# Two orders of issue in a fused two-block kernel: ScalarE's copies of the transposed probabilities set before the exponentials, and a broadcast matmul of the mLSTM core moved one unit ahead

## The chip, the cores and the metric

One core of one Trainium2 chip runs the whole program. The metric is the device time of one execution in microseconds (us); of the kernel before, the median of three runs is 4267.76 us (4265.85 to 4268.33).

The core has engines that run their own instruction streams and meet at semaphores: PE (TensorE, matrix products and transposes into PSUM), DVE (VectorE), ACT (ScalarE), POOL (GpSimd) and SP, which issues the loads from memory. Each engine starts its compute instructions in the order of its own stream; a wait at one instruction therefore holds back what stands behind it.

## The reference, cut to what matters

The input is 512 tokens of width 1024. A first block (a state-space branch, an RWKV branch, an HGRN branch, a feed-forward) runs once, then two layers of a second block. Each of those two layers has four branches on the normalised tokens, a gated merge, an output projection and a feed-forward. The change touches only the cores of the four branches:

```python
# A: mLSTM, 4 heads of 128, both directions, chunks of 128
dmat = where(lower, b[t] - b[s] + i[s], -inf);  mt = max(b + m, dmat.max(-1))
h = (q @ k.T * exp(dmat - mt)) @ v / max(abs(den), exp(-mt))        # forward + backward, then normed

# B: grouped-query attention, 8 heads of 64, 512 queries x 512 keys
p = softmax(q @ k.T);            o = p @ v
# C: neighbourhood attention, 8 heads, a window of 8 x 16 positions, with a bias table
p = softmax(q @ k.T + bias);     o = p @ v
# D: differential attention, 4 heads, two maps, a distance bias
a = softmax(s0) - lam * softmax(s1);   o = a @ v
```

Everything is held in 32-bit floats.

## The kernel before, in words

The program is a chain of stages. Long projection stages stream weights through SP and keep PE nearly full. Between them stand short stages without any weights, which work on tiles already in SBUF and PSUM; four of them per layer are meant here: the mLSTM core, and the cores of the grouped-query, differential and neighbourhood attentions (built by `gqa_attention`, `diff_attention`, `natten_branch`; each runs through `alone`, that is with nothing else beside it).

**An attention core** is a software pipeline over steps n. In a step, a block of 128 queries of two heads (and, in the differential one, of one of two maps) is handled. PE's stream for step n is: the scores of step n into PSUM (L3118, in the neighbourhood core L3379), then the transposes of the probabilities of an earlier pair (L3128, L3390), then the product with the values for one pair earlier still (L3140, L3401). DVE finds the row maxima of step n ("front": L3197; with a bias L3203 and L3208; L3449 and L3454), and then normalises step n-1 (L3175 to L3187; L3435, L3439). ACT computes the two exponentials of step n (L3156, L3415) and copies the transposed probabilities of the earlier pair from PSUM banks 4 and 5 into `prob_t` (L3163, L3423); this copy is called the take below. In the code m numbers the pairs whose probabilities are transposed, and m = n - 2, except in the differential core, where two maps make one m and it exists for every second n only.

The waits that tie these together: the scores of step n need the exponentials (or the front) of n-2 done; the transposes of m need its normalisation and the take of m-1, because they write the banks that the take reads; the values' product needs the take of m; the exponentials of n need the front of n; the take of m needs the transposes of m and the values' product of m-2. There are 16 steps in each of the three cores; the differential one has 8 transposed pairs.

**The mLSTM core** (`mlstm_branch`, L2922 on) runs 32 steps s in 8 units u of four (`NT` = 4); a unit is one head in one direction. At each unit's start PE spreads the unit's row of running maxima over all partitions with one 4x512 matmul into bank u % 2 ("spread", L2951). Per step: DVE bounds (spread value minus a column, L3031), ACT takes the exponential (L2991), POOL masks the diagonal block (L2971), PE makes the products of queries and keys (L2955), DVE multiplies the two ("weight", L3005), and PE multiplies that with the values ("weigh", L2933). In PE's stream, step s is: spread if s % 4 is 0, the query-key product of s (which needs the weight of s-2), weigh of s-2. In DVE's stream it is: bound of s, weight of s-2, and at s % 4 = 3 the closing of the previous unit (`finish`). The blocks of a unit have 512, 384, 256 and 128 columns, in this order.

The order of the work is written out in the source; no scheduler moves it.

Of the kernel before, what the change touches and what calls it, by code (L numbers as in the profile page):

```python
# [18 lines left out]
ACT = mybir.ActivationFunctionType  # L19
AX = mybir.AxisListType  # L20

P = 128
T = 512
NT = T // P
# [294 lines left out]
def bank(ps, b):  # L319
    return ps[:, b, :]  # L320
# [297 lines left out]
class Nothing:  # L618
# [10 lines left out]
    def scalar(self, act):  # L629
        yield  # L630
# [2241 lines left out]
def mlstm_branch(k, n_layer, y, o_gate, norm):  # L2872
# [7 lines left out]
    H, N, PAD = A_HEADS, 2 * A_WIDTH // P, A_CONV // 2  # L2880
    n = n_layer
    with ExitStack() as ctx:
# [8 lines left out]
        b_, g_, M_, m_ = [sb(name, [H, 2, T]) for name in ("b_rows", "g_rows", "max_rows", "m_rows")]  # L2891
        g_col, m_col = sb("g_cols", [P, NT, 2, H]), sb("floor_cols", [P, NT, 2, H])
        stat = sb("row_scale", [P, 2, NT])
# [5 lines left out]
        with ExitStack() as inner:  # L2899
# [8 lines left out]
            UNITS = 2 * H  # L2908
            STEPS = UNITS * NT

            def place(s):

                u = s // NT
                back, h = u % 2, u // 2
                j = NT - 1 - s % NT if back else s % NT
                return u, back, h, j, (slice(0, (j + 1) * P) if back else slice(j * P, T))

            def values(u, i):

                return k.ps[:, 4 + 2 * (u % 2) + i // 2, (i % 2) * (P + 1):(i % 2) * (P + 1) + P + 1]  # L2920

            @block.tensor  # L2922
            def _(pe):
                def weigh(s):
                    u, back, h, j, ts = place(s)
                    pe.wait_ge(prob_ready, s + 1)
                    if s % NT == 0 and u >= 2:
                        if back:
                            pe.wait_ge(y_ready, h)
                        else:  # L2930
                            pe.wait_ge(first_half, NT * h)
                    for i in range(0, j + 1) if back else range(j, NT):
                        mm = pe.matmul(values(u, i), dist[:, s % RING, i * P:(i + 1) * P], v_one[:, j, h, :],  # L2933
                                       start=(s % NT == 0 and i % 2 == 0), stop=(j == (0 if back else i)),
                                       skip_group_check=True)
                    mm.then_inc(pv_done, 1)

                def turn(h):

                    pe.wait_ge(both_halves, NT * (h + 1))  # L2940
                    for i in range(NT):
                        mm = pe.transpose(k.ps[:, 6, i * P:(i + 1) * P], tap[:, h % 2, i * P:(i + 1) * P],
                                          k.const("ident"))
                    mm.then_inc(turned, 1)

                for s in range(STEPS):
                    u, back, h, j, ts = place(s)
                    if s % NT == 0:
                        if u >= 2:
                            pe.wait_ge(bounded, NT * (u - 1))  # L2950
                        pe.matmul(bank(k.ps, u % 2), k.const("ident", H)[:, h:h + 1].broadcast_to([H, P]),  # L2951
                                  M_[:, back, :], start=True, stop=True).then_inc(spread, 1)
                    if s >= 2:
                        pe.wait_ge(prob_ready, s - 1)
                    pe.matmul(k.ps[:, 2 + s % 2, ts], qk[:, H + h, j * P:(j + 1) * P], qk[:, h, ts],  # L2955
                              start=True, stop=True).then_inc(qk_done, 1)
                    if s >= 2:
                        weigh(s - 2)
                    if s % NT == 0 and u >= 3 and back:
                        turn(h - 1)  # L2960
                weigh(STEPS - 2)
                weigh(STEPS - 1)
                turn(H - 1)
# [106 lines left out]
class Attention(Nothing):  # L3070
# [74 lines left out]
    def scalar(self, act):  # L3145
        k, stat = self.k, self.stat
        for n in range(self.N + 2):
            if n < self.N:
                g, i, c = self.place(n)
                act.wait_ge(self.fronts, self.front * (n + 1))  # L3150
                if n >= self.RE and self.bias_of is None:
                    act.wait_ge(self.turned, (n - self.RE) // self.maps + 1)
                for s in range(2):
                    at, e = 2 * (n % 4) + s, self.exp[:, n % self.RE, s, :]
                    src = bank(k.ps, 2 * (n % 2) + s) if self.bias_of is None else e
                    act.activation(e, src, ACT.Exp, bias=stat[:, 0, at:at + 1],  # L3156
                                   accum_out=stat[:, 1, at:at + 1]).then_inc(self.exps, 1)
            m = self.done(n - 2)
            if m is not None:
                act.wait_ge(self.turned, m + 1)  # L3160
                if m >= 2:
                    act.wait_ge(self.pv_done, m - 1)
                act.activation(self.pt[:, m % 2, :, :, :],  # L3163
                               k.ps[:, 4:6, :].rearrange("p s (j t) -> p s j t", j=NT), ACT.Copy).then_inc(self.taken, 1)
            yield

    def vector(self, dve):
# [172 lines left out]
class WindowAttention(Nothing):  # L3340
# [66 lines left out]
    def scalar(self, act):  # L3407
        k, stat = self.k, self.stat
        for n in range(self.N + 2):
            if n < self.N:  # L3410
                g, b, lo, w = self.place(n)
                act.wait_ge(self.fronts, 3 * (n + 1))
                for s in range(2):
                    at, e = 2 * (n % 4) + s, self.exp[:, n % self.RE, s, 0:w * P]
                    act.activation(e, e, ACT.Exp, bias=stat[:, 0, at:at + 1], accum_out=stat[:, 1, at:at + 1])\  # L3415
                        .then_inc(self.exps, 1)
            m = n - 2
            if m >= 0:
                g, b, lo, w = self.place(m)
                act.wait_ge(self.turned, m + 1)  # L3420
                if m >= 2:
                    act.wait_ge(self.pv_done, m - 1)
                act.activation(self.pt[:, m % 2, :, 0:w, :],  # L3423
                               k.ps[:, 4:6, 0:w * P].rearrange("p s (j t) -> p s j t", j=w), ACT.Copy)\
                    .then_inc(self.taken, 1)
            yield

    def vector(self, dve):
# [353 lines left out]
```

## Time and profile before

| | before |
|---|---|
| median of 3 runs | 4267.76 us |
| lowest, highest | 4265.85, 4268.33 us |
| profiled execution, its own time | 4268.34 us |
| its span | 4266.5 us |
| mean granted TensorE clock in it | 0.939 of full |
| PE busy | 3839.9 us (90%) |
| DVE busy | 2026.0 us (47%) |
| ACT busy | 1525.0 us (36%) |
| POOL busy | 399.8 us (9%) |

All times below are from that one execution. A busy share is a mean over stages with different limits, so the table says only that PE is the fullest engine of the program as a whole; the short stages have to be read one by one. In the profile a number in square brackets behind an instruction is the idle time of its engine just before it, with what ended it. Matrix products are pipelined and their ends are modelled; the distance between two starts is the better measure. A 32-bit product counts as two matmul records or more.

### The profile page before, as it was taken

The page shows a single profiled execution, that of the slowest core. Times are in us where ns is not written, and L with a number is a line of the kernel's source. Part 1 is how long each engine was busy: PE and PEld are TensorE (multiplying, and loading weights), DVE is VectorE, ACT ScalarE, POOL GpSimd, SP SyncE. Part 2 cuts the span into 40 slices and gives each one's busy share as a digit, 9 for nine tenths or more (in the row PEclk, how much of TensorE's full clock was granted, in tenths as well). Part 3 has the DMA queues.
Part 4 walks back from the last instruction along what each step waited for, and adds up shares of the span by engine and source line. Part 5 has one row for each costly group of instructions (what it writes and reads, how often), then busy time and mean ns, then how long its engine had stood idle before and what let it go on. Part 6 is the DMA issues. An engine that isn't in the chain of part 4 may idle for free. (4 is left out here: it accounts for less than half of the span.)

```text
span 4266.5 us, 51904 instructions
## 1 busy us (share of the span) xinstructions
PE 3839.9 (90%) x20480; PEld 2973.0 (70%) x20480; DVE 2026.0 (47%) x3134; ACT 1525.0 (36%) x2371; POOL 399.8 (9%) x356
## 2 busy tenths in 40 slices
PE   7888778969999998989789999999989789999998
PEld 5456667757878876766567877877766567777876
DVE  4867464485343333536546443333436645443332
ACT  4443312543332233424444332232424444233232
POOL 0025223000001103010000001100010000001100
PEclk9999778979999998999999999999999999999999
DMA  3011001202322222111112332222211112332222
GB/s 107 15 50 48 1 2 36 84 1 74 121 86 95 94 78 72 60 50 40 69 43 86 91 96 89 93 78 81 70 45 45 40 66 88 90 98 85 95 77 74
DMA packets 83486, 289.30 MB, mean 68 GB/s; under 512 B 9168, under 2 KB 9296, under 8 KB 82000
## 3 DMA queue, kind: packets, MB, share of 16 engines
q1 hardware_dynamic: 83136, 286.30, 20.9%
q8 instruction: 141, 2.31, 0.2%
q14 instruction: 65, 0.53, 0.0%
q10 hardware_dynamic: 144, 0.15, 0.0%
HBM read 284.32 MB, written 2.10 MB: 67 GB/s over the span
## 5 line engine op out<-in xcount | busy, mean ns | idle before, releaser
L547 DVE TENSOR_TENSOR weights_lo_r<-raw_weights,weights_hi_r 128x1024 fp32r<-128x1024 f32 (+2 forms) x554 | 633.0, 1143 | 1758.1 <-ACT weights_hi_r L541 1757.9
L541 ACT ACTIVATE weights_hi_r<-raw_weights 128x1024 fp32r<-128x1024 f32 (+2 forms) x554 | 548.0, 989 | 1856.8 <-PE ps L614 1821.3
L613 PE MATMUL ps<-xn_r,weights_hi_r 128*128 128x512 f32 x2816 | 1118.8, 397 | 0.0
L612 PE MATMUL ps<-xn_hi,weights_hi_r 128*128 128x512 f32 x1952 | 805.6, 413 | 74.4 <-DVE xn_r L607 27.3
L614 PE MATMUL ps<-xn_hi,weights_lo_r 128*128 128x512 f32 x1952 | 777.4, 398 | 0.0
L613 PEld LDWEIGHTS ps<-xn_r,weights_hi_r 128*128 128x128 f32 x2816 | 539.0, 191 | 126.7 <-issue 10.6
L612 PEld LDWEIGHTS ps<-xn_hi,weights_hi_r 128*128 128x128 f32 x1952 | 377.1, 193 | 193.9 <-issue 82.5
L614 PEld LDWEIGHTS ps<-xn_hi,weights_lo_r 128*128 128x128 f32 x1952 | 377.1, 193 | 83.6
L612 PE MATMUL ps<-y_r,weights_hi_r 128*128 128x512 f32 x1056 | 420.9, 399 | 1.6 <-PEq L858 1.6
L614 PE MATMUL ps<-y_r,weights_lo_r 128*128 128x512 f32 x1056 | 420.2, 398 | 0.0
L612 PE MATMUL ps<-hidden_hi,weights_hi_r 128*128 128x512 f32 x528 | 216.1, 409 | 31.9 <-DVE hidden_r L607 31.9
L612 PEld LDWEIGHTS ps<-y_r,weights_hi_r 128*128 128x128 f32 x1056 | 199.4, 189 | 50.6 <-issue 4.0
L614 PEld LDWEIGHTS ps<-y_r,weights_lo_r 128*128 128x128 f32 x1056 | 199.7, 189 | 49.3
L613 PE MATMUL ps<-hidden_r,weights_hi_r 128*128 128x512 f32 x528 | 214.9, 407 | 0.0
L614 PE MATMUL ps<-hidden_hi,weights_lo_r 128*128 128x512 f32 x528 | 214.3, 406 | 0.0
L1156 POOL TENSOR_TENSOR squares<-squares 128x512 f32<-128x512 f32 x18 | 23.2, 1291 | 1852.6 <-ACT squares L1145 1852.6
L612 PE MATMUL ps<-y_hi,weights_hi_r 128*128 128x512 f32 x384 | 157.1, 409 | 0.0
L614 PE MATMUL ps<-y_hi,weights_lo_r 128*128 128x512 f32 x384 | 151.9, 396 | 0.0
L613 PE MATMUL ps<-y_r,weights_hi_r 128*128 128x512 f32 x384 | 151.9, 396 | 0.0
L3627 POOL TENSOR_TENSOR y<-y 128x512 f32<-128x512 f32 x66 | 85.2, 1291 | 675.2 <-ACT y L3599 675.2
L612 PEld LDWEIGHTS ps<-hidden_hi,weights_hi_r 128*128 128x128 f32 x528 | 103.0, 195 | 60.6 <-DVE weights_lo_r L547 20.0
L614 PEld LDWEIGHTS ps<-hidden_hi,weights_lo_r 128*128 128x128 f32 x528 | 102.9, 195 | 25.3
(490 smaller groups left out, 5340.0 us busy)
## 6 DMA issues: line engine op xcount, KB each, us to landing
raw_weights<-in_w_ffn_dram SPq DMA_DIRECT2D x132, 512.0 KB, 3.7
raw_weights<-in_w_down_dram SPq DMA_DIRECT2D x48, 512.0 KB, 3.5
raw_weights<-in_w_out_dram SPq DMA_DIRECT2D x24, 512.0 KB, 3.5
bias_table<-in_window_bias_dram SPq DMA_DIRECT2D x8, 1280.0 KB, 10.5
raw_weights<-in_w_down_dram SPq DMA_DIRECT2D x24, 384.0 KB, 3.1
raw_weights<-in_w_hgrn_dram SPq DMA_DIRECT2D x16, 512.0 KB, 3.5
raw_weights<-in_w_mix_ssm_dram SPq DMA_DIRECT2D x16, 512.0 KB, 3.7
raw_weights<-in_w_a_qk_dram SPq DMA_DIRECT2D x16, 512.0 KB, 3.4
```

The lines of the kernel that those rows point to most:

```text
L541: act.activation(self.k.w_hi[:, g % 2, 0:chunk.width], self.k.raw[:, slot, 0:chunk.width], ACT.Copy)\
L547: dve.tensor_tensor(self.k.w_lo[:, g % 2, 0:chunk.width], self.k.raw[:, slot, 0:chunk.width], self.k.w_hi[:, g % 2, 0:chunk.width].bitcast ...
L612: pe.matmul(out, w_hi, x_hi, start=start, stop=False)
L613: pe.matmul(out, w_hi, x_lo, start=False, stop=False)
L614: return pe.matmul(out, w_lo, x_hi, start=False, stop=stop)
L1156: pool.tensor_tensor(self.sums[:, n, :], self.sums[:, n, :], self.sq[:, kinds * (m % 2) + n, :], ALU.add)\
L3627: pool.tensor_tensor(gate[:, s, :], gate[:, s, :], rstd, ALU.mult).then_inc(gate_scaled, 1)
```

## The change

Two edits.

In both attention classes, `scalar` (ACT's stream) has its two parts exchanged inside a step: first the take of m, then the exponentials of step n. Nothing else in the two classes changes, neither a wait nor a number that is waited for.

In the mLSTM core the spread of unit u+1 is issued in the middle of unit u, behind the weigh of s - 2 at s % 4 = 2, and no longer in front of the first query-key product of unit u+1. The spread of unit 0 stands before the loop. The wait for the bank's last reader (`bounded`) goes along.

```diff
+                def spread_maxima(u):
+                    if u >= 2:
+                        pe.wait_ge(bounded, NT * (u - 1))
+                    pe.matmul(bank(k.ps, u % 2), k.const("ident", H)[:, u // 2:u // 2 + 1].broadcast_to([H, P]),
+                              M_[:, u % 2, :], start=True, stop=True).then_inc(spread, 1)
+
+                spread_maxima(0)
                 for s in range(STEPS):
                     u, back, h, j, ts = place(s)
-                    if s % NT == 0:
-                        if u >= 2:
-                            pe.wait_ge(bounded, NT * (u - 1))
-                        pe.matmul(bank(k.ps, u % 2), k.const("ident", H)[:, h:h + 1].broadcast_to([H, P]),
-                                  M_[:, back, :], start=True, stop=True).then_inc(spread, 1)
                     if s >= 2:
                         pe.wait_ge(prob_ready, s - 1)
                     pe.matmul(k.ps[:, 2 + s % 2, ts], qk[:, H + h, j * P:(j + 1) * P], qk[:, h, ts],
                               start=True, stop=True).then_inc(qk_done, 1)
                     if s >= 2:
                         weigh(s - 2)
+                    if s % NT == 2 and u + 1 < UNITS:
+                        spread_maxima(u + 1)
...
     def scalar(self, act):
         k, stat = self.k, self.stat
         for n in range(self.N + 2):
+            m = self.done(n - 2)
+            if m is not None:
+                act.wait_ge(self.turned, m + 1)
+                if m >= 2:
+                    act.wait_ge(self.pv_done, m - 1)
+                act.activation(self.pt[:, m % 2, :, :, :],
+                               k.ps[:, 4:6, :].rearrange("p s (j t) -> p s j t", j=NT), ACT.Copy).then_inc(self.taken, 1)
             if n < self.N:
                 g, i, c = self.place(n)
                 act.wait_ge(self.fronts, self.front * (n + 1))
...
-            m = self.done(n - 2)
-            if m is not None:
-                act.wait_ge(self.turned, m + 1)
-                if m >= 2:
-                    act.wait_ge(self.pv_done, m - 1)
-                act.activation(self.pt[:, m % 2, :, :, :],
-                               k.ps[:, 4:6, :].rearrange("p s (j t) -> p s j t", j=NT), ACT.Copy).then_inc(self.taken, 1)
             yield
```

The same exchange is made in `WindowAttention.scalar`, with the take of w blocks instead of four.

On ACT, at the start of the first grouped-query core (L3156 the exponentials, two to a step; L3163 the take), the kernel before has:

```order
L3156 ACTIVATE exps,statistics<-ps,statistics 128x512 x6
L3163 ACTIVATE prob_t<-ps 128x1024
L3156 ACTIVATE exps,statistics<-ps,statistics 128x512 x2
L3163 ACTIVATE prob_t<-ps 128x1024
L3156 ACTIVATE exps,statistics<-ps,statistics 128x512 x2
```

and the changed one, in which the exponentials are L3167 and the take is L3157:

```order
L3167 ACTIVATE exps,statistics<-ps,statistics 128x512 x4
L3157 ACTIVATE prob_t<-ps 128x1024
L3167 ACTIVATE exps,statistics<-ps,statistics 128x512 x2
L3157 ACTIVATE prob_t<-ps 128x1024
L3167 ACTIVATE exps,statistics<-ps,statistics 128x512 x2
```

The first take stands behind the exponentials of two steps instead of three, and every later one has moved ahead of one step's pair of exponentials.

On PE, around the boundary between the first and the second unit of the mLSTM core (L2951 the spread, L2955 the query-key products, L2933 the weigh), the kernel before has:

```order
L2955 MATMUL ps<-qk 128x256
L2933 MATMUL ps<-v_tok,qk_raw 128x129 x4
L2955 MATMUL ps<-qk 128x128
L2933 MATMUL ps<-v_tok,qk_raw 128x129 x3
L2951 MATMUL ps<-max_rows,consts 128x512
L2955 MATMUL ps<-qk 128x512
L2933 MATMUL ps<-v_tok,qk_raw 128x129 x2
```

and the changed one (L2949 the spread, L2957 the query-key products):

```order
L2957 MATMUL ps<-qk 128x256
L2933 MATMUL ps<-v_tok,qk_raw 128x129 x4
L2949 MATMUL ps<-max_rows,consts 128x512
L2957 MATMUL ps<-qk 128x128
L2933 MATMUL ps<-v_tok,qk_raw 128x129 x3
L2957 MATMUL ps<-qk 128x512
L2933 MATMUL ps<-v_tok,qk_raw 128x129 x2
```

The spread has moved up past one 128-column product and three weigh products, which now stand between it and the 512-column product.

## Rows read from the trace of the kernel before

**Rows 1.** Windows; columns: stretch, length, busy (xcount) of PE, PEld, DVE, ACT, POOL, PEclk, DMA share, GB/s
```profile
1819.50:1822.50 3.00, 3.00 (x10) 2.20 (x9) 1.92 (x8) 0.31 (x1) 0.94 (x3) 0.50 0.00 0
1990.00:2036.00 46.00, 40.75 (x366) 26.14 (x364) 30.63 (x57) 31.82 (x70) 0.00 (x0) 1.00 0.01 1
2066.00:2068.00 2.00, 2.00 (x10) 1.77 (x10) 0.00 (x0) 0.00 (x0) 0.00 (x0) 0.50 0.00 0
2073.11:2087.49 14.38, 10.39 (x65) 6.64 (x65) 11.13 (x31) 7.81 (x18) 0.00 (x0) 1.00 0.00 1
2199.78:2210.38 10.60, 8.66 (x77) 5.42 (x77) 7.90 (x35) 7.15 (x20) 0.00 (x0) 1.00 0.01 2
```

**Rows 2.** Timeline, mLSTM core, a unit boundary; columns: start, length, engine, line, instruction
```profile
1793.32 0.39 PE L2955 MATMUL ps<-qk 128*128 128x128 f32 x2
...
1794.30 1.12 PE L2951 MATMUL ps<-max_rows,consts 4*128 4x512 f32 x2
1795.46 0.75 DVE L3031 TENSOR_SCALAR qk_raw<-ps,g_cols 128x512 f32<-128x512 f32 x1 [2.64 <-PE ps L2951]
1796.13 0.41 DVE L3005 TENSOR_TENSOR qk_raw<-qk_raw,ps 128x256 f32<-128x256 f32 x1
...
1796.59 1.12 PE L2955 MATMUL ps<-qk 128*128 128x512 f32 x2 [1.17 <-DVE qk_raw L3005]
```

**Rows 3.** Timeline, PE alone, later unit starts of the mLSTM core
```profile
1803.47 1.13 PE L2955 MATMUL ps<-qk 128*128 128x512 f32 x2 [1.17 <-DVE qk_raw L3005]
...
1817.96 1.13 PE L2955 MATMUL ps<-qk 128*128 128x512 f32 x2 [1.17 <-DVE qk_raw L3005]
1826.51 1.12 PE L2955 MATMUL ps<-qk 128*128 128x512 f32 x2 [1.17 <-DVE qk_raw L3005]
```

**Rows 4.** Timeline, grouped-query core, two steps
```profile
1999.21 1.07 PE L3128 MATMUL ps<-consts,exps 128*128 128x128 f32 x8 [0.71 <-ACT prob_t L3163]
...
2002.32 1.07 PE L3128 MATMUL ps<-consts,exps 128*128 128x128 f32 x8
...
2003.67 0.69 ACT L3156 ACTIVATE exps<-ps,statistics 128x512 f32<-128x512 f32 x1 [1.50 <-DVE statistics L3197]
...
2005.01 1.02 ACT L3163 ACTIVATE prob_t<-ps 128x1024 f32<-128x1024 f32 x1
...
2005.52 1.23 DVE L3197 TENSOR_REDUCE statistics<-ps 128x2 f32<-128x1024 f32 x1 [0.89 <-PE ps L3118]
...
2006.18 1.07 PE L3128 MATMUL ps<-consts,exps 128*128 128x128 f32 x8 [0.70 <-ACT prob_t L3163]
```

**Rows 5.** Who waited for the take (us, times), both layers: L3163
```profile
  PE ps L3140: 28.1, 14
  PE ps L3128: 13.5, 18
```

**Rows 6.** The same for the neighbourhood core's take: L3423
```profile
  PE ps L3390: 13.7, 22
```

**Rows 7.** Timeline, differential core, one pair of steps
```profile
2076.27 0.69 DVE L3203 CUSTOM_DVE_ANT_0 exps<-ps,distance_bias 128x512 f32<-128x512 f32 x1 [1.49 <-PE ps L3118]
...
2079.24 1.00 ACT L3163 ACTIVATE prob_t<-ps 128x1024 f32<-128x1024 f32 x1
...
2080.30 2.05 PE L3140 MATMUL ps<-prob_t,d_v 128*128 128x128 f32 x16 [2.00 <-ACT prob_t L3163]
...
2080.56 1.42 DVE L3187 SCALAR_TENSOR_TENSOR exps<-exps,statistics 128x512 f32<-128x512 f32 x2
```

**Rows 8.** Timeline, PE alone, differential core: the products with the values of two earlier pairs
```profile
2064.32 3.24 PE L3140 MATMUL ps<-prob_t,d_v 128*128 128x128 f32 x16 [1.99 <-ACT prob_t L3163]
2073.11 2.05 PE L3140 MATMUL ps<-prob_t,d_v 128*128 128x128 f32 x16 [2.00 <-ACT prob_t L3163]
```

**Rows 9.** What DVE's fronts of the differential cores waited for (us, times): L3203
```profile
  PE ps L3118: 25.8, 16
```

**Rows 10.** Timeline, neighbourhood core, the transposes that open a group of four steps
```profile
2199.78 0.63 PE L3390 MATMUL ps<-consts,exps 128*128 128x128 f32 x4 [1.02 <-ACT prob_t L3423]
```

More of the change, by code:

```diff
@@ L3409, in scalar @@
         for n in range(self.N + 2):
[L3410 to L3416, printed above, removed]
             m = n - 2
@@ L3425, in scalar @@
                     .then_inc(self.taken, 1)
+            if n < self.N:
+                g, b, lo, w = self.place(n)
+                act.wait_ge(self.fronts, 3 * (n + 1))
+                for s in range(2):
+                    at, e = 2 * (n % 4) + s, self.exp[:, n % self.RE, s, 0:w * P]
+                    act.activation(e, e, ACT.Exp, bias=stat[:, 0, at:at + 1], accum_out=stat[:, 1, at:at + 1])\
+                        .then_inc(self.exps, 1)
             yield
```

## The prediction, made before the changed kernel was run

> **What bounds the kernel now.** I began with the table of engines and the forty slices: PE is 90% busy over the whole, but the slices with the low digits are those in which almost nothing is loaded. Those are the cores without weights, and the edits touch only them. So I went on to the windows [rows 1]. In the steady part of the grouped-query core PE works 40.75 of 46 us; in the differential core 10.39 of 14.38, in the neighbourhood core 8.66 of 10.60. All three have free time on every engine at once (DVE 30.63, 11.13, 7.90), which means a ring of waits and not a full engine. The timelines then say which wait ends last.
>
> In the mLSTM core it is the start of a unit [rows 2]: the spread starts at 1794.30, DVE has stood idle 2.64 us for it, bounds at 1795.46, weights at 1796.13, and only then may PE go on, at 1796.59, after 1.17 us of idleness. The same 1.17 us stand before the first product of each of the 14 units that follow another unit (7 in each layer) [rows 2, 3].
>
> In the grouped-query core [rows 4] PE has transposed by 2002.32 + 1.07 = 2003.4, but the take starts at 2005.01, because ACT first runs the exponentials of the step, which could start only at 2003.67. The next transposes, at 2006.18, have waited 0.70 us for that take, as every second one does. In the differential core the product with the values waits 2.00 us [rows 7]; in the neighbourhood core transposes wait, 1.02 us at most and 1.94 us in a group of four steps, the stretch's 10.60 minus PE's 8.66 [rows 1, 10].
>
> **The change, part by part.** No instruction is added and none is removed; no DMA, no queue of SP or POOL is passed. The sums below are waits that go.
>
> *mLSTM core.* The chain from the spread's start to the 512-column product is 1796.59 - 1794.30 = 2.29 us [rows 2], and the change keeps it: DVE's bound still needs the spread, its weight still follows the bound. But one 128-column product and three weigh products now run inside it. Before, they ran from 1793.32 to 1794.30, 0.98 us [rows 2]. The spread itself occupies PE about as long as from 1794.30 to 1796.59 less the idle 1.17, so 1.12. PE is then ready at 1.12 + 0.98 = 2.10, the chain at 2.29: about 0.2 us of the 1.17 stays. Saved: 0.98 per boundary, 14 x 0.98 = 13.7 us. What is late next is DVE's closing of a backward unit, which stands before the bound; I followed one such boundary through and it frees DVE within 0.1 us of the spread's end, so I charge nothing. If that cover is gone, its cost is a few tenths at 6 boundaries, 2 us. The bounds are 0 (if the middle of a unit has no slack for the spread) and 14 x 1.17 = 16.4.
>
> *The clock in that core.* From 1819.50 to 1822.50 the granted clock is 0.50, that is 1.2 GHz instead of 2.4 [rows 1], and the unit in it takes 1826.51 - 1817.96 = 8.55 us against 1803.47 - 1796.59 = 6.88 for one of its size [rows 2, 3]: 1.67 us for a dip. Three units of the two layers show one. In the differential core a dip stands between 2064.32 and 2073.11, 8.79 us against 7.19 for the next pair (2080.30 - 2073.11): 1.6 us [rows 7, 8], four of them in steady state. In the grouped-query core the granted clock is 1.00 throughout 46 us in which PE is 89% busy [rows 1]. With the waits gone, both other cores come to that density or above it: in the mLSTM core only 0.2 us in some 5.9 stay idle. I count two of the three dips there as gone: 2 x 1.67 = 3.3 us, with the bounds 0 and 5.0.
>
> *Grouped-query core.* The take moves to where the transposes end. The exponentials then start after it: transposes' end 2003.4 + 1.02 = 2004.4 instead of 2003.67, 0.75 us later. They are needed by DVE's normalisation, which stands behind the next front. The exponentials end at 2005.8 (they took 2005.01 - 2003.67 = 1.34); DVE's next front waits for the next scores and runs from 2005.52 to 2006.75, so 0.9 us of slack is left. PE becomes the bound, with (6.97 - 0.70) / 2 = 3.13 us a step. ACT's own load is 1.34 + 1.02 = 2.36, below it. The waits before L3128 sum to 13.5 us in 18 places [rows 5]. The last of each layer, 1.02 and 0.18, stand where no exponentials are left and stay: 11.0 us. Bounds 0 and 13.5.
>
> *Differential core.* PE waits 28.1 us in 14 places [rows 5], but PE is not what decides here once the take is early. DVE does four things for a pair: from 2076.27 to the end of L3187, 2080.56 + 1.42 = 2081.98, it works without a gap for 5.71 us, and waits 1.49 before it [rows 7]. PE needs, with rows 8's distance, 7.19 - 2.00 = 5.19. So a pair falls from 7.19 to 5.71. The fronts' waits in both layers sum to 25.8 us in 16 places [rows 9]; I leave out some 5 us for the filling of the pipeline, in which nothing has been transposed yet, and 1.6 us for one dip that stays: 19.2 us. The slack in the ring is thin. With X the end of L3187, transposes run to about X + 1.2 (1.07 and a start), the take to X + 2.2 (1.00), the exponentials to X + 3.6 (1.34, rows 4). DVE wants them when front, normalisation and front are done, which is 5.71 less the 1.42 of L3187 and some 0.45 of small work before it, X + 3.8. Bounds 14.4 (all four dips stay) and 22.8 (the filling costs 3 instead of 5).
>
> *Neighbourhood core.* PE waits 13.7 us in 22 places [rows 6]. PE needs 8.66 us for a group of four steps and DVE, waits inside it left out, 7.90 [rows 1]; with the small gaps between dependent instructions I add up 8.3. The margin is 0.4 us a group. I take 10.0 us, with the bounds 0 and 12.5 (the 13.7 without those of the tails and of a start at half clock).
>
> Sum: 13.7 + 3.3 + 11.0 + 19.2 + 10.0 = 57.2 us. The profiled execution took 4268.34 us, of which 4266.5 are its span; that is 0.6 above the median of the runs, so the median becomes 4267.8 - 57.2 = 4211 us, 1.3% less.
>
> A rule of the Trainium skill speaks against the exchange. What the trace shows first: the take stands 1.6 us behind the end of its transposes, with ACT at work on what precedes it in the stream [rows 4]. "TensorE: Matmul & The Clock Gate", Part 1, says that ScalarE and VectorE take their instructions strictly first in, first out. The trace agrees. By that rule the exchange has its price: the exponentials now cannot pass a take that waits for PE. That price is the 0.75 us above; it costs nothing while the slack of 0.9 us holds, and by the rule alone, without slack, it would be 0.75 x 16 x 2 = 24 us in the grouped-query core.
>
> **The rivals.** *The clock keeps its dips.* For it: dips also stand behind stretches whose PE work is mostly transposes and small products, and these stay. Against it: the grouped-query core, with the same transposes, has none in 46 us [rows 1]. Price: 3.3 us in the mLSTM core, and in the differential core 19.2 - 14.4 = 4.8. Time 4211 + 8.1 = 4219.
>
> *The thin margins fail.* DVE or ACT becomes the bound in the neighbourhood core, with latencies that I have not seen between take and exponentials: 0.4 us a step less gained there over 16 steps in two layers takes all 10.0, and 0.3 us in each of some 12 pairs of the differential core takes 3.6. Time 4211 + 13.6 = 4225. For it: ACT's 7.15 us of a group are 1.8 of a step that would be 8.66 / 4 = 2.17, and each of its two waits adds a start. Against it: nothing says that these starts take more than the 0.4 left.
>
> *Covered.* Something else sets the pace of those stages, and the time stays at 4268. Only a record that names the wrong releaser could bring this; the take and the waiting transposes line up to 0.15 us [rows 4], in each of 18 places.
>
> *Slower.* The exponentials, held behind a take that waits for PE, close a ring at half clock. At 0.50 each PE step doubles from 3.13 to 6.26 us, the take and with it the exponentials come later by the same factor, so all cores run at PE's half pace. Place: the grouped-query core, whose steady part shows no dip now. Price: 3.13 us a step. It takes 57.2 / 3.13 = 18 of its 32 steps at half clock to lose all of the gain; with all 32, 100 us are lost and the time is 4311. For it: the clock does fall in cores of this kind [rows 1]. Against it: it fell where PE was idle more, and the change makes it idle less.
>
> **How the numbers follow.** Chances: my forecast 0.60, dips kept 0.18, margins fail 0.15, covered 0.03, slower 0.04. The forecast's own range is 4203 to 4216: with all dips gone and nothing lost the terms are 13.7 + 5.0 + 11.8 + 22.8 + 12.5 = 65.8, which gives 4202. The range that holds 8 in 10 goes from there through both middle cases and a little past the second: 4202 to 4227. About 0.2%, 8.5 us, is what a measurement of this kernel can tell from no change; faster by more than that are the first three cases, 0.93; same 0.03; slower 0.04.
>
> **What would show it right or wrong.** In the profile of the changed kernel: (1) the idle before the 512-column query-key product falls from 1.17 to about 0.2, and a unit's start follows the last one after some 5.9 us instead of 6.88; (2) in the grouped-query core no transposes wait for the take in steady state, and their distance is 3.13 us; (3) in the differential core the fronts no longer wait for PE, and a pair takes 5.7 us; (4) the neighbourhood core's group takes 8.7 to 9.0 us; (5) the granted clock is 1.00 in steady state in all four. It is wrong if exponentials are now what DVE waits for, if (3) stays above 6.3, or if stages outside these eight change by more than 1 us.

## The result, and the profile after

| | before | after |
|---|---|---|
| median | 4266.81 us (4 runs) | 4189.91 us (4 runs) |
| lowest, highest | 4260.96, 4268.33 | 4186.72, 4195.19 |
| profiled execution, its own time | 4268.34 | 4195.19 |
| its span | 4266.5 | 4193.4 |
| mean granted TensorE clock | 0.939 | 0.943 |

The ratio is 0.983, with the 95% interval 0.981 to 0.984: faster, by 77 us. I had predicted 4211 with the range 4202 to 4227; the time lies 12 us below its low end. The sign was right, the size was not.

The profiled executions differ by 73.15 us. I cut both at the borders of the stages. The eight cores account for 69.35 us of it, all other stages together for 3.8. For each core, in us: its length; the time in it in which PE is not busy; and the time at half clock, worked out as 2 x (1 - granted clock) x length. A stretch at half clock is called a dip. The granted clock is printed with two digits, so the last figure is good to about 0.6 us (2 x 0.005 x 60): 7.4 against 6.7, or 3.8 against 3.4, is no difference. In the trace's own record of the clock the grouped-query cores have 6.8 and 3.2 us of half clock in both orders.

| core (layer) | length | PE not busy | half clock | shorter by | forecast, both layers |
|---|---|---|---|---|---|
| mLSTM (1) | 62.77 to 55.40 | 11.05 to 3.37 | 7.5 to 5.5 | 7.4 | |
| mLSTM (2) | 66.12 to 56.05 | 11.05 to 3.37 | 14.6 to 7.8 | 10.1 | 17.0, was 17.4 |
| grouped-query (1) | 61.51 to 55.41 | 8.69 to 2.83 | 7.4 to 6.7 | 6.1 | |
| grouped-query (2) | 61.30 to 54.63 | 9.52 to 3.09 | 3.7 to 3.3 | 6.7 | 11.0, was 12.8 |
| differential (1) | 69.89 to 57.17 | 20.05 to 12.88 | 21.0 to 6.9 | 12.7 | |
| differential (2) | 66.97 to 56.43 | 20.05 to 12.88 | 13.4 to 3.4 | 10.5 | 19.2, was 23.3 |
| neighbourhood (1) | 47.77 to 39.47 | 9.26 to 5.03 | 10.5 to 0 | 8.3 | |
| neighbourhood (2) | 47.05 to 39.47 | 10.88 to 5.04 | 3.8 to 0 | 7.6 | 10.0, was 15.9 |

The cores of layer 1 in the windows before (mLSTM, grouped-query, differential, neighbourhood; columns as in [rows 1]):

```profile
1787.71:1850.48 62.77, 51.72 (x256) 35.29 (x257) 37.50 (x104) 22.06 (x53) 14.30 (x32) 0.94 0.00 1
1982.23:2043.74 61.51, 52.82 (x448) 33.43 (x449) 37.37 (x68) 39.27 (x81) 0.00 (x0) 0.94 0.00 1
2043.74:2113.63 69.89, 49.84 (x257) 32.91 (x257) 46.88 (x140) 31.53 (x72) 0.00 (x0) 0.85 0.00 1
2182.92:2230.69 47.77, 38.51 (x304) 24.06 (x305) 31.67 (x132) 28.98 (x81) 0.00 (x0) 0.89 0.00 1
```

and after, followed by one group of four steps of the neighbourhood core and one pair of the differential core:

```profile
1788.06:1843.46 55.40, 52.03 (x256) 35.02 (x257) 37.44 (x104) 22.01 (x53) 14.25 (x32) 0.95 0.00 1
1973.93:2029.34 55.41, 52.58 (x448) 33.41 (x449) 37.53 (x68) 39.14 (x81) 0.00 (x0) 0.94 0.00 1
2029.34:2086.51 57.17, 44.29 (x257) 28.17 (x257) 46.49 (x140) 31.58 (x72) 0.00 (x0) 0.94 0.00 1
2155.73:2195.20 39.47, 34.44 (x305) 21.83 (x305) 31.18 (x132) 29.55 (x81) 0.00 (x0) 1.00 0.01 1
2170.48:2179.47 8.99, 8.60 (x77) 5.42 (x77) 7.72 (x34) 7.38 (x21) 0.00 (x0) 1.00 0.00 1
2051.28:2056.89 5.61, 5.26 (x33) 3.32 (x33) 5.43 (x18) 3.95 (x9) 0.00 (x0) 1.00 0.00 0
```

The reader should compare PE's busy column. The instructions are the same, yet PE is busy 5.55 us less in the differential core and 4.07 us less in the neighbourhood core: the same products took less time, because less of them ran at half clock. Such a gain is not a wait that goes; it stands in no list of waits.

In the mLSTM core the boundary that answers to [rows 2] reads, in the timeline:

```profile
1800.89 1.12 PE L2949 MATMUL ps<-max_rows,consts 4*128 4x512 f32 x2
1801.94 0.49 PE L2957 MATMUL ps<-qk 128*128 128x128 f32 x2
1802.05 0.75 DVE L3035 TENSOR_SCALAR qk_raw<-ps,g_cols 128x512 f32<-128x512 f32 x1 [1.49 <-PE ps L2949]
...
1802.71 0.41 DVE L3009 TENSOR_TENSOR qk_raw<-qk_raw,ps 128x256 f32<-128x256 f32 x1
...
1803.18 1.13 PE L2957 MATMUL ps<-qk 128*128 128x512 f32 x2
```

The chain from the spread's start is 1803.18 - 1800.89 = 2.29 us, as before to the hundredth. PE now works inside it; the bracket with 1.17 us is gone. The next unit starts at

```profile
1809.16 1.13 PE L2957 MATMUL ps<-qk 128*128 128x512 f32 x2
1815.59 1.12 PE L2957 MATMUL ps<-qk 128*128 128x512 f32 x2
```

so 5.98 and 6.43 us for the two kinds of unit; in [rows 2, 3] the first kind took 6.88, and both together 14.49 (1817.96 - 1803.47), now 12.41.

A step of the grouped-query core:

```profile
2001.68 1.09 PE L3132 MATMUL ps<-consts,exps 128*128 128x128 f32 x8
2001.80 1.22 DVE L3201 TENSOR_REDUCE statistics<-ps 128x2 f32<-128x1024 f32 x1 [0.89 <-PE ps L3122]
...
2002.81 1.02 ACT L3157 ACTIVATE prob_t<-ps 128x1024 f32<-128x1024 f32 x1 [0.75 <-PE ps L3132]
...
2003.73 0.68 ACT L3167 ACTIVATE exps<-ps,statistics 128x512 f32<-128x512 f32 x1
...
2004.78 1.09 PE L3132 MATMUL ps<-consts,exps 128*128 128x128 f32 x8
```

The step is 3.10 us and no transpose waits. ACT now waits 0.75 us for PE before the take. The exponentials behind it become ready while the take runs, at 2003.02, where their front (started at 2001.80) ends, and start at 2003.73. In this step nobody waits for them. In the whole profile the normalisations wait for exponentials in 6 places, 4.0 us together (before: 4 places, 1.5 us); none of the 6 lies in a steady stretch.

A stretch of the differential core:

```profile
2056.75 0.68 DVE L3207 CUSTOM_DVE_ANT_0 exps<-ps,distance_bias 128x512 f32<-128x512 f32 x1
2056.89 1.09 PE L3132 MATMUL ps<-consts,exps 128*128 128x128 f32 x8 [0.29 <-DVE exps L3191]
...
2058.02 1.02 ACT L3157 ACTIVATE prob_t<-ps 128x1024 f32<-128x1024 f32 x1 [1.41 <-PE ps L3132]
...
2059.10 2.05 PE L3144 MATMUL ps<-prob_t,d_v 128*128 128x128 f32 x16
```

The take that [rows 7] have at 2079.24, 1.06 us ahead of the product that waited 2.00 us for it, now follows the transposes at once. DVE's front has no bracket: the list of what the fronts (L3207) waited for has 6.1 us in 6 places, where [rows 9] have 25.8 in 16. DVE is busy 5.43 of 5.61 us and is what bounds the pair.

### The profile page after: what moved, and what is told of

Same layout as the page of the kernel before. It is cut to its first block and busy times, and to the rows that moved or that the text cites. A ratio compares the mean times of both kernels' runs of the same rounds, so it can differ in the third digit from the quotient of the medians.

```text
span 4193.4 us, 51904 instructions
## 1 busy us (share of the span) xinstructions
PE 3822.6 (91%) x20480; PEld 2960.6 (71%) x20480; DVE 2024.4 (48%) x3134; ACT 1524.8 (36%) x2371; POOL 399.6 (10%) x356
## 5 line engine op out<-in xcount | busy, mean ns | idle before, releaser
L1156 POOL TENSOR_TENSOR squares<-squares 128x512 f32<-128x512 f32 x18 | 23.3, 1294 | 1797.2 <-ACT squares L1145 1797.2
```

What stands on the lines that cost most here:

```text
L1156: pool.tensor_tensor(self.sums[:, n, :], self.sums[:, n, :], self.sq[:, kinds * (m % 2) + n, :], ALU.add)\
```

## The experiments

Two theories stood at first. **A**: each core's gain is its own, namely the waits that went and, where PE is fuller, the full clock that it then keeps. **B**: the half clock has nothing to do with the waits; it comes and goes by chance or with the stage, and the excess over the forecast is something else.

### One core at a time: e1, e2, e3, e4

Each starts from the kernel before and takes one part of the change. e1 has only the hunk of `mlstm_branch`. In e2 and e3 the attention class asks which core it is (one map: grouped-query, two: differential), and e4 changes `WindowAttention.scalar` alone:

```diff
         for n in range(self.N + 2):
+            if self.maps == 1:          # e2; in e3: self.maps == 2
+                take(n)
             ...                         # the exponentials of n
+            if not (self.maps == 1):
+                take(n)
```

> The mLSTM edit alone, the three attention cores as before. Theory A (each core's gain is its own: fewer waits, and a fuller PE that keeps the full clock in that core): the two mLSTM cores lose 15.4 us of PE idle time and about 2 us of half clock, together 17 us, and the six attention cores keep their old idle time (8.7 to 20.1 us each) and, on average, their old half clock (before: 21.0 and 13.4 us in the differential cores, 10.5 and 3.8 in the neighbourhood ones). Total 4250 us. Theory B (half clock comes and goes by chance from one execution to the next, whatever the order of the work): untouched cores show 0 half clock in some of them, the neighbourhood cores above all, and the total may be anywhere within 4245 to 4256.

> The exchange of take and exponentials in the grouped-query core alone. Theory A: these two cores lose 12.3 us of PE idle time, half clock in them stays where it was (at their start), the others are as before; total 4267 - 12.5 = 4254 us. Theory B: the same for the idle time, and the untouched cores' half clock scatters, down to 0 in some. Under both, transposes of this core follow each other by 3.13 us in steady state, and the differential core behind it is no shorter than 66 us.

> The exchange in the differential core alone. Theory A: idle time falls by 14.3 us in the two cores and the half clock in each falls from 21.0 and 13.4 us to below 8, which is worth another 8.9 us of PE time; together 23 us, total 4244 us. Theory B: the idle time falls by 14.3 us, and the half clock falls only by chance: 4 to 20 us remain in a core, and the total is 4246 to 4253.

> The exchange in the neighbourhood core alone. Theory A: idle time falls by 10.1 us and the half clock goes from 10.5 and 3.8 us to 0 in both cores, 16 us together, total 4251 us, and both cores take 39.5 us. Theory B: the idle time falls by 10.1 us, some half clock shows in at least one of the two cores, and the total is 4253 to 4257.

| | median, us | ratio (95%) | its two cores | shorter by | half clock there |
|---|---|---|---|---|---|
| e1 | 4236.0 | 0.994 (0.992 to 0.996) | 54.97, 56.05 | 17.9 | 4.4, 7.8 |
| e2 | 4247.2 | 0.996 (0.995 to 0.997) | 54.63, 55.41 | 12.8 | |
| e3 | 4235.9 | 0.994 (0.992 to 0.996) | 57.49, 57.58 | 21.8 | 6.9, 6.9 |
| e4 | 4248.8 | 0.997 (0.996 to 0.998) | 39.47, 39.48 | 15.9 | 0, 0 |

The before on that chip had a median of 4266.3. "Shorter by" is against the cores of the profile of before. Its sum is 68.4; the whole change gave 69.35. So the gains of the cores add up, and each stands in the core whose order was changed.

Part of what B says is true all the same. In untouched cores the half clock moves between profiles too: e2's first differential core had 10.7 us instead of 21.0 (66.95 us long instead of 69.89), e3's first neighbourhood core 3.8 instead of 10.5, e4's second mLSTM core 7.6 instead of 14.6. A single pair of profiles can't price the clock. All profiles together can. The old order had 10.7 to 21.1 us of half clock in ten differential cores, the new one 3.4 to 6.9 in twelve (e7's, which have spare products, left out); in the neighbourhood core it is 3.8 to 10.5 in eight against 0 in eleven of twelve. These ranges do not meet, and no untouched core of the two kinds came down to 0, which is against B. In the mLSTM core they just meet: 7.4 to 15.4 in twelve against 4.9 to 7.7 in eight (from the clock's record). With the mean over all profiles of either order in place of the one pair (kernels that alter a core in some other way are left out for that core), the eight cores give 68.6 us instead of 69.35: 52.8 of PE's time not busy, and 15.8 of its busy time (mLSTM 3.1, grouped-query 0.4, differential 7.8, neighbourhood 4.4).

The medians did not come out as A had them: they lie 14, 7, 8 and 2 us below its totals (4250, 4254, 4244, 4251). Nor do they add up: 30.3 + 19.1 + 30.4 + 17.5 = 97.3 for a whole of 77. The profiles show one reason for unsteady totals: the stretch of the first block from about 262 us on, 700 us long and touched by no edit, took 716.9 us in the profile of before, 716.7 after, and 714.4, 707.6, 710.0 and 707.7 in e1 to e4. It goes with half clock: by the clock's record the two longest of these stretches had 249.5 and 254.0 us of it, those of e2 and e4 233.5. What makes the half clock differ there I did not find. Cores are therefore compared by their lengths, in which e6, a repeat of the changed kernel, differs from it by 0.4 us at most. The old order scatters more: its ten differential cores took 66.95 to 70.21 us, its twelve mLSTM cores 62.77 to 66.63.

### The clock by itself: e5

The kernel before, with spare products into banks that nothing reads before they are overwritten, at places where PE waits. The order of takes and exponentials stays, so the waits for the take stay.

```diff
+                if maps == 2:                 # differential: ahead of the wait for the take
+                    for r in range(6):
+                        pe.matmul(self.out(2 * g + r % 2)[:, i * P:(i + 1) * P], self.v_of(2 * g + r % 2, 0), k.const("ident"), start=True, stop=True)
                 pe.wait_ge(self.taken, m + 1)
...
+                if n >= 3:                    # neighbourhood: four products of 128 columns, behind the scores
+                    ...
```

> The kernel before, with spare products put into PE's idle time: four 128-column ones in each step of the neighbourhood core, between the scores and the transposes, and six in each pair of the differential core, ahead of the wait for the take; their results are overwritten. All waits and the order of the real work stay. They add about 0.5 us of PE time to a step and 1.5 us to a pair, in places where PE stands idle. Theory A (the clock falls where PE stands idle much, and the part of the gain that the removed waits don't explain is the clock that the fuller PE keeps): half clock falls from 3.8-10.5 us to 0 in each neighbourhood core, and from 10.7-21.1 to below 8 in each differential one; the differential cores get shorter by 3 to 5 us each in spite of the added work (67-70 to 64-66), the neighbourhood cores by 0 to 4. Theory B (the clock has nothing to do with it, the waits alone made the gain): no core gets shorter, half clock stays at the values of before, and the added work makes the cores 0 to 3 us longer.

Median 4258.0 against 4263.6, ratio 0.998 (0.997 to 0.999). The differential cores took 66.78 and 66.68, with 6.7 us of half clock each, where the old order had 10.7 to 21.1 in ten cores of five profiles. The pair stayed at 7.18 us. Windows of that core and the neighbourhood core of e5:

```profile
2037.41:2104.19 66.78, 55.51 (x352) 39.69 (x353) 46.88 (x140) 31.50 (x72) 0.00 (x0) 0.95 0.00 1
2173.43:2221.67 48.24, 44.71 (x408) 28.74 (x409) 31.67 (x132) 28.93 (x81) 0.00 (x0) 0.93 0.01 2
```

and PE's timeline:

```profile
2059.46 2.05 PE L3147 MATMUL ps<-prob_t,d_v 128*128 128x128 f32 x16 [0.45 <-ACT prob_t L3170]
2066.64 2.05 PE L3147 MATMUL ps<-prob_t,d_v 128*128 128x128 f32 x16 [0.46 <-ACT prob_t L3170]
```

The reader sees PE 5.67 us busier than before and this core 3.11 us shorter, with no dip in the steady part; the dip that is left begins ahead of the first spare product. The waits for the take end where they did, so it is the filling of PE's idle time that kept the clock: for the half clock in the differential core A holds. For the length it holds less well. A had 64 to 66 us, and 66.7 came out; five of the ten cores of the old order took 66.95 to 66.97 us, so against these only 0.2 to 0.3 us are gained. Part of the reason is that the first six spare products had no wait to fill: they ran at half clock and put off the product with the values by 2.44 us (2049.93 to 2052.37). Against the mean of the ten, 68.26, the two cores gain 3.1 us; clock and waits together gave 23.3. In the neighbourhood core the test missed: 6.8 us at half clock in both layers, begun before the first spare product, and the cores took 48.24 and 48.21 us. It decides nothing on that core.

### The whole change again, and with warmed starts: e6, e7

e6 is the changed kernel once more. e7 adds spare products of 512 columns, four before the mLSTM core and five ahead of the first transposes of the differential core. Of its edit only the second part is shown:

```diff
+            if m == 0 and maps == 2:
+                for _ in range(5):
+                    pe.matmul(bank(k.ps, 6), self.q_of(0, 0)[:, 0:P], self.k_of(0, 0), start=True, stop=True)
```

> The changed kernel once more, beside the others on one chip. Expected 4190 us; the eight changed cores as before (55.4 and 56.1, 55.4 and 54.6, 57.2 and 56.4, 39.5 and 39.5 us, each within 1.5), the long stretch of the first block, from 263 to 980 us, anywhere between 707 and 717 us.

> The changed kernel with spare products in two places where PE still stands idle: four of 512 columns at the end of the projection ahead of the mLSTM core, in the 4.4 us that PE waits there, and five in the 3.3 us ahead of the first transposes of the differential core. Theory A: the half clock at the start of the mLSTM cores (5.5 and 7.9 us, in which PE is full) goes, worth 2.8 to 3.9 us of each core, and that in the differential cores (6.9, 3.4) goes too, worth 1 to 2 each; together 7 to 10 us, 4181 us. Theory B: nothing gained, 4190 us, or up to 2 us lost where the spare products delay the first real ones.

e6: 4184.2, ratio 0.981 (0.980 to 0.982); its cores lie within 0.4 us of those above, the neighbourhood cores 39.47 and 39.48. e7: 4183.2, ratio 0.982 (0.980 to 0.984). The starts did change: the mLSTM cores had 3.3 and 0 us at half clock (54.46 and 54.11 us), the differential ones 0 and 3.4 (55.90 and 57.23), the 3.4 near the core's end. Against e6 these four cores gained 3.2 us, where A had 7 to 10. And the first neighbourhood core, whose code it does not touch, had a dip of 6.7 us that began 4.6 us after its start, and took 42.04. All eight cores together took 414.0 us in e7 and 413.9 in e6, and the total is no better than e6's. A dip at a core's start comes and goes between profiles of kernels that are alike in that core.

### Where the spread stands: e8, e11

From the changed kernel, the spread of the next unit one step later (ahead of the last weigh of the unit), or one step earlier:

```diff
-                    if s % NT == 2 and u + 1 < UNITS:
+                    if s % NT == 3 and u + 1 < UNITS:   # e8, ahead of weigh(s - 2)
+                    if s % NT == 1 and u + 1 < UNITS:   # e11, at the same place in the step
```

> The changed kernel, with the spread of the next unit one product later: at s % 4 = 3, between the 128-column query-key product and the weigh behind it. The chain theory (spread start to 512-column product is always 2.29 us, and what PE runs inside it is what is saved): only three weigh products, 0.75 us, lie inside it now instead of 1.0, so the idle before the 512-column product is 0.4 to 0.5 us instead of 0.2, and each mLSTM core takes 7 x 0.25 = 1.8 us more than in the changed kernel, 57.2 and 57.9. The rival (any place ahead of the boundary does as well, since DVE is what is late): no difference.

> The changed kernel, with the next unit's spread one step earlier still (s % 4 = 1). The chain theory: the 2.29 us from the spread to DVE's weight are then wholly inside PE's other work, the last 0.08 us of PE idle time and the hold of 0.2 us at each boundary go, a unit takes 5.8 instead of 5.98 us at full clock, and each mLSTM core is shorter by 7 x 0.2 = 1.4 us; total 4184 - 3 = 4181 us. The rival (DVE and the closing of a backward unit are late next): no difference, 4184 us.

e8: 4191.9, ratio 0.983 (0.981 to 0.985); the mLSTM cores 57.16 and 57.68 instead of 55.40 and 56.05. Its boundary, on PE:

```profile
1796.05 1.12 PE L2949 MATMUL ps<-max_rows,consts 4*128 4x512 f32 x2
...
1798.34 1.13 PE L2957 MATMUL ps<-qk 128*128 128x512 f32 x2 [0.30 <-DVE qk_raw L3009]
...
1804.55 1.13 PE L2957 MATMUL ps<-qk 128*128 128x512 f32 x2 [0.30 <-DVE qk_raw L3009]
```

The chain is 2.29 us a third time, and the wait is what the work inside does not cover; it is 0.30 us, a little less than the 0.4 to 0.5 expected, and the cores came out as the chain theory had them. e11: 4183.7, ratio 0.981 (0.980 to 0.983), the mLSTM cores 52.54 and 55.08. In the cores that is 3.5 us less than e6's 55.04 and 56.04, more than the 2.8 expected: the two kinds of unit took 5.64 and 6.07 us instead of 5.98 and 6.43, while PE's time not busy fell by only 0.6 us a core. Where the rest comes from is open. The total cannot be told from e6's 4184.2, and the two ran on different chips. So the place between is not the best one for the core, and nothing here beats the changed kernel by a measurable amount.

### The neighbourhood core's 3.8 us: e9, e10

e5 had missed there, so a third theory, **C**: the dip behind the pipeline's start hangs on one wait. In the second layer of the kernel before, PE's second group of transposes stood behind the first take:

```profile
3477.72 1.19 PE L3390 MATMUL ps<-consts,exps 128*128 128x128 f32 x6 [1.78 <-ACT prob_t L3423]
```

and after, in both layers, behind a normalisation and shorter:

```profile
2161.49 0.87 PE L3394 MATMUL ps<-consts,exps 128*128 128x128 f32 x6 [0.72 <-DVE exps L3443]
```

e9 is the kernel before with this first take alone (n = 2) ahead of the exponentials; e10 the changed kernel with this take alone behind them.

```diff
+            if n == 2:                        # e9;  in e10: if n != 2
+                take(n)
             ...                               # the exponentials of n
+            if not (n == 2):
+                take(n)
```

> The kernel before, with only the first take of the neighbourhood core ahead of its step's exponentials (n = 2); the other 15 stay behind. Theory C (the half clock of 3.8 us in this core stands behind one wait, that of the second pair's transposes for the first take, 1.78 us at full clock, and goes with it): the wait falls to about 0.7 us and the core has 0 half clock, or 6 to 8 us where a dip begins at its very start; never 3.8. A core without a dip takes about 47.0 - 1.1 - 1.9 = 44.0 us. Theory A (the share of idle time over the steady steps decides): the steady steps have their old waits, so 3.8 to 10.5 us of half clock stay, and the core takes 46 us or more. Total 4256 to 4260 us under C, 4262 under A.

> The changed kernel, with only the first take of the neighbourhood core put back behind its step's exponentials. Theory C: the wait of 1.78 us and with it the half clock of about 3.8 us come back in both cores; each takes 39.5 + 1.0 + 1.9 = 42.4 us. Theory A: the half clock stays at 0, and each core takes 40.5 us. Total 4190 us under C, 4186 under A.

e9: 4258.9 against 4261.3, ratio 0.9995 (0.9986 to 1.0004), not to be told from no change. e10: 4189.5, ratio 0.983 (0.981 to 0.984). What counts is in the cores. The windows of e9:

```profile
2176.09:2221.32 45.23, 34.60 (x304) 21.85 (x305) 31.56 (x132) 28.82 (x81) 0.00 (x0) 1.00 0.00 1
3458.55:3504.24 45.69, 37.28 (x304) 23.34 (x305) 31.65 (x132) 28.82 (x81) 0.00 (x0) 0.93 0.01 1
```

and of e10, with its second group of transposes on PE:

```profile
2147.98:2190.05 42.07, 35.97 (x304) 22.77 (x305) 31.18 (x132) 29.54 (x81) 0.00 (x0) 0.96 0.00 1
3400.27:3442.30 42.03, 35.93 (x305) 22.72 (x305) 31.19 (x132) 29.53 (x81) 0.00 (x0) 0.96 0.00 1
```

```profile
2154.80 1.44 PE L3394 MATMUL ps<-consts,exps 128*128 128x128 f32 x6 [1.78 <-ACT prob_t L3421]
```

One take put back brings the wait back (1.78 us) and with it 3.4 us of half clock in both layers, and costs 2.6 us a core: 42.07 and 42.03 against 39.47, of which 1.1 is PE standing idle longer and 1.5 is PE's busy time. Up to that wait the two kernels run alike: in both PE is busy 3.55 of the core's first 5.04 us (2147.98 to 2153.02 in e10, 2155.73 to 2160.77 in the changed kernel). Then it stands idle 1.78 us in one and 0.72 in the other, so it is the one wait that makes the difference. One take moved gives the old order a core at full clock throughout; its other core had a dip of 6.4 us, begun 1.3 us after its start, ahead of any take. Both cores took under the 46 us that A wanted at least. For the half clock C holds; for the length of e9 it does not: the core without a dip took 45.23 us and not 44.0, since PE's time not busy was 10.62 us, hardly less than 10.88 before. The wait for the first take went, and others grew.

C explains the dips that begin some 7 us after the core's start, which five of the eight cores of the old order had. In the other three, the first-layer core of the kernel before with its 10.5 us among them, the dip began 1.5 to 4.6 us after the start, ahead of the wait for the first take. Why is open, as it is for the one in e7. Over all profiles, the old order had 3.8 to 10.5 us at half clock in each of eight neighbourhood cores; the new order had none in 11 of 12.

## Why the prediction was wrong

**The waits were right.** Test by test: (1) PE's idle before the 512-column product fell from 1.17 to 0.1 instead of 0.2, the unit takes 5.98 where I had said 5.9. (2) 3.10 us a step, said 3.13, with no wait of a transpose. (3) 5.61 us a pair, said 5.7. (4) 8.99 us a group, said 8.7 to 9.0. Of the 57.2 us, 49.1 were waits (all but the 8.1 of the clock, which the first rival names); PE's time not busy in the eight cores fell by 52.1: mLSTM 15.4, grouped-query 12.3, differential 14.3, neighbourhood 10.1. The surplus in the mLSTM core is mostly that the chain leaves 0.1 us of each boundary's 1.17 and not 0.2: 14 x 1.07 is 15.0. In the grouped-query core no transpose waits for the take any more, not even the last ones of a layer, which I had left standing.

**The step that failed is the price of the clock.** The sum had 3.3 us for it in the mLSTM core ("I count two of the three dips there as gone"), 4.8 us in the differential core, and nothing at all in the other two; the neighbourhood core's 10.0 us are waits alone. Priced were 8.1 us; PE's busy time fell by 17.3: mLSTM 2.1, grouped-query 0.5, differential 8.9, neighbourhood 5.8. The excess of 9.2 us lies in two cores, 4.1 in the differential and 5.8 in the neighbourhood one, less 1.2 by which the mLSTM core was priced too high. With the means over all profiles it is 15.8 against 8.1: 3.0 too little in the differential core and 4.4 in the neighbourhood one. For the neighbourhood core I had not asked what its 10.5 and 3.8 us at half clock stood behind, though its mean clock of 0.89 was to be had in the same view as [rows 1]; e9 and e10 show that the 3.8 stood behind a single wait of the class that I was removing, worth 1.5 us of PE's time a core. That the 10.5 went is not shown to be the change's doing: they began ahead of that wait. Test (5) came out right: after the change the half clock stands only at the starts (1788 to 1794, 1975 to 1982 and 2036 to 2043 us in the first layer), but for 0.8 us at the end of the second mLSTM core, and the steady parts are at 1.00.

**The range was cut too low at its far end for the same reason.** My best case, 65.8 us, still had the neighbourhood core's dips in it; the cores gave 69.35. It also did not use the bounds that I had given: with 16.4 and 13.5 us for the waits of the mLSTM and grouped-query cores in place of 13.7 and 11.8 (a figure that stands nowhere else) it would have been 70.2, and the low end 4198. That holds what the cores gave, but not the measured 4190.

**The rest was luck, and is partly open.** Of the 20.7 us by which the median beat 4210.6 (4267.8 - 57.2), 12.2 are in the cores. 3.8 are outside them: the merge behind the second neighbourhood core took 336.1 instead of 338.6 us, a projection behind the mLSTM core 40.9 instead of 42.2. I had said that more than 1 us there would prove me wrong. Less half clock fell in both, and for the merge this may be the change's doing: behind the second neighbourhood core it took 336.1 to 336.9 us in six of the seven profiles with the new order of that core (339.1 in the seventh) and 338.1 to 338.7 in all five with the old one. Behind the first neighbourhood core no such difference shows, and no run tests it. The last 5 us are that the changed kernel's profiled execution was the slowest of its four runs, 5.3 above their median. What made the others faster is open.

**The rivals.** The clock did not keep its dips (half-clock time in the eight cores fell from 81.9 to 33.6 us). The margins held: the exponentials start 0.71 us behind their front's end where I had said 0.75, the slack of 0.9 us covered it, and the grouped-query cores gained 12.8 us. The strict order of ScalarE's instructions, which the Trainium skill states ("TensorE: Matmul & The Clock Gate", Part 1), is seen in that delay; the loss of 24 us that it would mean without slack is not. No ring closed at half clock: the grouped-query cores have as much half clock as before, and got shorter.

## What to carry to other kernels

Where an engine takes its work in order and has two jobs in a step, put first the one for which the scarcest engine waits, once the job put back has slack; the timeline gives the slack, and here sums of such waits came out within 3 us in 49. Then read the granted clock of every short stage and find the wait ahead of each fall: a wait that goes can take with it half-clock time that stands in no list of waits, and here that was about a quarter of the gain (17.3 of 69.35 us in one pair of profiles, 15.8 of 68.6 on the mean of all). Judge edits of a few us by the lengths of their stages in the profile, since an untouched stretch of this program differed by 9 us between profiles.

## What the runs showed of the hardware that I had not expected

- The granted clock fell from 2.4 to 1.2 GHz behind a wait of 1.78 us of PE, where PE had been busy 3.55 of the 5.04 us before it, and did not fall when that wait was 0.72 (e10 and the changed kernel, two cores each). The half clock behind it lasted 3.4 us and cost 1.5 us of PE's time; the longer wait itself cost 1.1.
- Spare products in PE's waits took the dips out of a stage's steady part, though they make PE busier: 6.7 us at half clock in both differential cores of e5, 10.7 to 21.1 in ten without them. The stage got no longer by the added work: 66.78 and 66.68 us against 66.95 to 70.21.
- Dips at the start of a stage come and go between profiles of like kernels: one of 6.7 us stood at a neighbourhood core of e7 and in none of the other eleven of its order. Of the eight cores of the old order three had such a dip.
- A chain over three engines (a 4x512 product, DVE's bound, DVE's weight, the next product) took 2.29 us in three orders of issue, with no product, three weigh products, or these and a 128-column product run in between (before, e8, after).
